# A two-layer decoder trunk on one core: feature stages that begin on two turned tiles, mixer output kept in SBUF, and the last chunk computed half by half

## The chip, the cores and the metric

The kernel runs on one core of one Trainium2 chip. The metric is the time of one execution in device microseconds (us). The kernel before was run three times: 2418.59 us median, 2418.29 to 2418.76. Results differ by less than 0.02% from run to run here.

## The reference, cut to what matters

The input is one sequence of 256 tokens, 2048 wide, f32. Two layers follow one another, and each is three residual steps, every one with an RMS norm before it and one behind it:

```
for i in range(2):
    hn = rms_norm(h, pre_mix_g[i])
    y = conformer_conv(hn, ...) if i == 0 else diff_attention(hn, ...)
    h = h + rms_norm(y, post_mix_g[i])
    f = conv_ffn(rms_norm(h, pre_ffn_g[i]), ...)          # 2048 -> 2 x 5632 -> 2048
    h = h + rms_norm(f, post_ffn_g[i])
    gate = sigmoid(rms_norm(h, ple_pre_g[i]) @ w_gate[i] + b_gate[i])
    h = h + rms_norm(gate * (p[i] @ w_proj[i]), ple_post_g[i])
return h
```

All products are computed from f32 weights (some 447 MB are read) to nearly f32 accuracy.

## The kernel before, in words

**Products.** A weight unit is 256 rows by 512 columns. SyncE loads it into one of four raw slots (RING = 4). ScalarE casts it to `w_hi` (`split` of the scalar block, L625), VectorE makes the rest `w_lo = raw - w_hi` (`split` of the vector block, L1021), and TensorE multiplies three times: high by high, high by low, low by high. A unit that has been multiplied frees its slot (`units_used`). The activations `x` have a high and a low part too.

**Two kinds of stage.** In a token stage (pw2, wo, down, gate, gates) the output has tokens on partitions: per unit two halves of 128 tokens with six matmuls each (`token_unit`, L1642 to L1644), and 8 units (22 in down) fill the two banks of a chunk of 512 columns. In a feature stage (up0, qk, up1) the output has features on partitions: `feature_chunk` with `product(j)` runs over the 8 units j of a chunk, each with 2 input tiles kt and 4 feature blocks, 16 matmuls in all (L1607 and L1609), into four of the eight PSUM banks, 0 to 3 for the first chunk.

**The turn into a stage.** The stages come one after the other and each starts from the new `h`. At the end of a mixer or embedding step, ScalarE sums squares (L663), VectorE applies the bias (L1120) and the gain (`times_gain`, L1058) and reduces the sums (L1037, L1039), and GpSimd takes the power -1/2 (L561). Then `residual` on VectorE updates `h` in eight pieces of 128 tokens by 512 columns (L1066), TensorE turns `h` into 16 tiles of 128 features by 256 tokens in PSUM (`turn_h`, L1587, two transposes of 128x128 a tile), ScalarE makes the high parts (`x_high`, L655), and VectorE the low parts (`x_low`, L1046). There are three turns into a feature stage: mix0 to up0, ple0 to qk, mix1 to up1. In these tile kt lies at position kt, two to a bank, so tiles 0 to 7 lie in banks 0 to 3, where the first chunk's products go. So the first chunk begins when four tiles are ready, multiplies two units for blocks 0 and 1 alone (their banks hold tiles 0 to 3), and goes on when eight tiles are ready:

```
early = 2
pe.wait_ge(x_ready, KT * LEFT[left] + 4)
for j in range(early):
    product(j, (0, 1))
```

Tiles 8 to 15 are turned inside the first chunk, after product 1 (mix) or 2 (qk). The mixer's chunk 0 of output is kept in SBUF (`y_first`) and its other three chunks stay in PSUM until the residual has read them. While the norm is worked out, `keep_warm` runs 17 (mix0) or 13 (mix1) small matmuls on TensorE (L1699).

**The statistic.** The norm's scale is applied after the product, so the stage begins without it. The squares of `h` (`h_squares`, L647) are summed on ScalarE, VectorE reduces them (`inverse_root`), GpSimd takes the root, VectorE writes two diagonals (`rstd_diagonals`, L1107), and TensorE spreads them over all partitions (`spread_statistic`, L1594), after product 5 in the up stages and after product 6 in qk. `turn_p` (L1904) turns the rows of p after product 4. All these stand in the engines' queues, in the order in which `new_h` (mix to up) and `new_h_behind` (ple0 to qk) write them, between the casts and splits of units 3 to 7.

**The end.** In the last gate chunk (gates1) both halves of a unit are multiplied before the next unit. Then `gate_post` works on halves 0 and 1, both roots are taken in one instruction, and of the eight pieces of the output five are updated on VectorE (`ON_DVE`, L1066) and three on TensorE and ScalarE (`ON_PE` = 3, 5, 7: `ident` by `h` plus `diag` by `z`, L1957 and L1962, copied at L1002). SyncE (L536) and ScalarE (L1004) issue a store of 256 KB for each piece. Ten more keep-warm matmuls (END_WARM) stand before the diagonals' products.

## Time and profile before

| what | us |
|---|---|
| median of 3 runs | 2418.59 |
| the profiled execution's own time | 2418.1 |
| its span, first to last instruction | 2416.3 |
| TensorE busy | 2398.6 (99%) |
| VectorE busy | 1638.4 (68%) |
| ScalarE busy | 1238.3 (51%) |

A timeline's row gives start, duration, engine, line, operation, the tiles written and read, how many instructions it merges (x8), and in brackets the idle time of the engine before it with what ended it. "issue" there means that nothing in the profile shows what the engine waited for. PE is TensorE, DVE VectorE, ACT ScalarE, POOL GpSimd, SPq and ACTq the queues that issue DMAs. Merged instructions overlap: the last of x8 ends at the row's end, and the step from one to the next is (duration - one instruction) / 7.

### The profile page before, as it was taken

What the parts mean: (1) busy time and instruction counts of PE and PEld (TensorE: products, weight loads), DVE (VectorE), ACT (ScalarE), POOL (GpSimd) and SP (SyncE); (2) the same over time, 40 slices, a digit from 0 to 9 for tenths busy, and PEclk for the clock granted to TensorE, in tenths of its full rate; (3) what the DMA queues carried; (4) which work ended last, traced back from release to release, by engine and by line L of the source; (5) the groups of instructions that cost most, each with busy time, mean ns of one, the idle gap of its engine ahead of it and who ended that gap; (6) DMA issues with size and microseconds to landing.
All of it is one profiled execution on the core that took longest, in us unless ns stands there. A gap on an engine that the chain in (4) does not pass through costs nothing.

```text
span 2416.3 us, 38816 instructions
## 1 busy us (share of the span) xinstructions
PE 2398.6 (99%) x12372; PEld 2057.9 (85%) x12372; DVE 1638.4 (68%) x2223; ACT 1238.3 (51%) x1777; POOL 36.1 (1%) x65
## 2 busy tenths in 40 slices
PE   9999999999999999999999999999999999999999
PEld 8888788888888888888888888888888888888887
DVE  6999767777777754447755676577777777644475
ACT  3433645555555544446644455465656656444463
POOL 2000000000000000000000000000000000000000
PEclk9999999999999999999999999999999999999999
DMA  8552546656656665566576544646566656656563
GB/s 268 181 165 90 175 148 205 187 180 198 191 182 191 196 209 195 193 199 227 176 212 201 183 150 156 193 155 192 183 190 196 187 182 197 212 187 200 194 234 135
DMA packets 370942, 452.48 MB, mean 187 GB/s; under 512 B 27460, under 2 KB 279494, under 8 KB 369440
## 3 DMA queue, kind: packets, MB, share of 16 engines
q1 hardware_dynamic: 367456, 435.54, 56.8%
q0 software_dynamic: 2960, 15.02, 1.8%
q8 instruction: 44, 0.72, 0.1%
q10 hardware_dynamic: 432, 0.79, 0.1%
q14 instruction: 50, 0.41, 0.1%
HBM read 447.05 MB, written 4.19 MB: 187 GB/s over the span
## 4 chain that ended last, share of the span: by engine, by line
PE 94%; issue 3%; DVE 1%; ACT 0%; DMA 0%; SPq 0%; POOL 0%; ACTq 0%; POOLq 0%; DVEq 0%
PE ps L1607 31%; PE ps L1609 16%; PE ps L1642 12%; PE ps L1643 12%; PE ps L1644 12%; PE ps L1692 9%; PE ps L1587 1%; PE ps L1856 0%; PE ps L1842 0%; DVE h L1066 0%; PE ps L1785 0%; PE ps L1793 0%; DMA h<-in_x 0%; PE ps L1572 0%; POOL rstd L561 0%
## 5 line engine op out<-in xcount | busy, mean ns | idle before, releaser
L1021 DVE TENSOR_TENSOR w_lo<-raw,w_hi 128x1024 fp32r<-128x1024 f32 x758 | 923.6, 1224 | 627.7 <-ACT w_hi L625 621.8
L625 ACT CAST w_hi<-raw 128x1024 fp32r<-128x1024 f32 x758 | 791.0, 1049 | 721.6 <-PE ps L1644 365.7
L1607 PE MATMUL ps<-x,w_hi 128*128 128x512 f32 x3328 | 1155.5, 391 | 4.1 <-issue 4.1
L1609 PE MATMUL ps<-x,w_lo 128*128 128x256 f32 x3328 | 931.7, 280 | 0.0
L1607 PEld LDWEIGHTS ps<-x,w_hi 128*128 128x128 f32 x3328 | 622.4, 187 | 141.2 <-issue 4.7
L1609 PEld LDWEIGHTS ps<-x,w_lo 128*128 128x128 f32 x3328 | 628.9, 189 | 0.0
L1644 PE MATMUL ps<-w_hi,mid 128*128 128x512 f32 x704 | 273.9, 389 | 0.0
L1643 PE MATMUL ps<-w_lo,mid 128*128 128x512 f32 x704 | 273.9, 389 | 0.0
L1642 PE MATMUL ps<-w_hi,mid 128*128 128x512 f32 x704 | 273.9, 389 | 0.0
L1642 PE MATMUL ps<-w_hi,x 128*128 128x512 f32 x640 | 253.2, 396 | 0.0
L1644 PE MATMUL ps<-w_hi,x 128*128 128x512 f32 x640 | 249.3, 389 | 0.0
L1643 PE MATMUL ps<-w_lo,x 128*128 128x512 f32 x640 | 249.2, 389 | 0.0
L1692 PE MATMUL ps<-xn,wg 128*128 128x256 f32 x896 | 193.7, 379 | 0.0
L1692 PEld LDWEIGHTS ps<-xn,wg 128*128 128x128 f32 x896 | 170.2, 190 | 23.1
L1462 DVE SCALAR_TENSOR_TENSOR acc<-ext,cols,acc 128x256 f32<-128x256 f32 x352 | 147.2, 480 | 46.0 <-ACT acc L931 39.6
L1644 PEld LDWEIGHTS ps<-w_hi,mid 128*128 128x128 f32 x704 | 132.2, 188 | 27.7
L1642 PEld LDWEIGHTS ps<-w_hi,mid 128*128 128x128 f32 x704 | 132.2, 188 | 27.4
L1643 PEld LDWEIGHTS ps<-w_lo,mid 128*128 128x128 f32 x704 | 132.2, 188 | 27.2
L1644 PEld LDWEIGHTS ps<-w_hi,x 128*128 128x128 f32 x640 | 120.1, 188 | 25.3
L1642 PEld LDWEIGHTS ps<-w_hi,x 128*128 128x128 f32 x640 | 120.2, 188 | 25.0 <-issue 0.4
L1643 PEld LDWEIGHTS ps<-w_lo,x 128*128 128x128 f32 x640 | 120.2, 188 | 24.5 <-issue 0.2
L1188 DVE SCALAR_TENSOR_TENSOR acc<-u_ext,wconv,acc 128x256 f32<-128x256 f32 x322 | 133.9, 477 | 1.2 <-ACT acc L750 1.1
(193 smaller groups left out, 1297.7 us busy)
## 6 DMA issues: line engine op xcount, KB each, us to landing
raw<-in_ffn_w_in SPq DMA_DIRECT2D x704, 256.0 KB, 3.2
raw<-in_ffn_w_out SPq DMA_DIRECT2D x352, 256.0 KB, 3.5
raw<-in_attn_w_qkv SPq DMA_DIRECT2D x192, 256.0 KB, 2.9
raw<-in_ple_w_gate SPq DMA_DIRECT2D x128, 256.0 KB, 3.7
wg<-in_conv_w_pw SPq DMA_DIRECT2D x112, 256.0 KB, 3.9
raw<-in_conv_w_pw SPq DMA_DIRECT2D x64, 256.0 KB, 3.6
raw<-in_attn_w_o SPq DMA_DIRECT2D x64, 256.0 KB, 3.5
wg<-in_conv_w_pw SPq DMA_DIRECT2D x32, 128.0 KB, 4.2
```

What stands on the lines that cost most here:

```text
L625: nc.scalar.copy(w_hi[:, u % RING], raw[:, u % RING]).then_inc(hi_split, 1)
L1021: nc.vector.tensor_tensor(w_lo[:, u % RING], raw[:, u % RING], w_hi[:, u % RING].bitcast(F32), ALU.subtract).then_inc(split_done, 1)
L1188: step.mark(nc.vector.scalar_tensor_tensor(both[:, a], u_ext[:, p, tap:tap + T], wconv[:, tap * KT + p:tap * KT + p + 1], nshift[:] if tap ...
L1462: ins = nc.vector.scalar_tensor_tensor(acc[:, f], ext[:, f, tap:tap + T], col(f"ffn_tap{layer}{tap}", c * 2 + (f if f < 2 else FT + f - 2) ...
L1587: ins = nc.tensor.transpose(tiles[:, turned_at(left, kt), P * half:P * (half + 1)], h[:, half, P * kt:P * (kt + 1)], ident[:])
L1607: mm(ps[:, 4 * s + f], w_hi[:, u % RING, q, columns], x[:, kt].rearrange("p a t -> p (a t)"), start=kt == 0, stop=False)
L1609: ins = mm(ps[:, 4 * s + f, 0:T], w_lo[:, u % RING, q, columns], x[:, kt, 0], start=False, stop=kt == KT - 1)
L1642: mm(bank(half), hi, w_hi[:, u % RING, q], start=first, stop=False)
L1643: mm(bank(half), hi, w_lo[:, u % RING, q], start=False, stop=False)
L1644: ins = mm(bank(half), lo, w_hi[:, u % RING, q], start=False, stop=last)
L1692: ins = mm(ps[:, 4 * (c % 2) + f, 0:T], wg[:, glu_slot(u), q, P * f:P * (f + 1)], source[:, kt], start=kt == 0, stop=kt == KT - 1)
```

## The change

Feature stages (mix0 to up0, ple0 to qk, mix1 to up1; the set `ALONE`):
- Tiles 0 to 11 lie one to a bank in banks 4 to 7, and tiles 12 to 15 in banks 4 and 5. Tiles 4 to 7 use the places of 0 to 3, tiles 8 to 11 again the same.
- The first residual chunk is done in four instructions of 256 columns instead of two of 512; TensorE turns tiles 0 and 1, then 2 and 3 (`turn_begun`). Product 0 waits for two ready tiles, and product j for 2j+2. There is no early part any more.
- The other tiles are turned in three groups of four inside the first chunk, behind products 0, 2 and 4 (`turn_rest`), each once the places are free.
- `new_h` becomes `new_h_quick` with another order of residuals, low parts, squares, casts and splits, and qk uses it too. In up stages `turn_p` moves behind product 5.
- All of the mixer's output goes to SBUF (`y_mix`). In pw2's last chunk VectorE leaves two splits, not one, for behind the chunk.
- The early projections of layer 1 use banks 0 to 3, and both are copied before the stage begins. MIX_WARM is (15, 13).

The kernel's end:
- The last four units of the last chunk are multiplied for half 0 first, then for half 1.
- Sigmoid, gating, squares, root, diagonal and residuals are done for half 0, then for half 1. Two roots of one column each replace one of two. The gain's product is written to `sig`.
- `ON_PE` is (0, 2, 1), `ON_DVE` is (4, 6, 3, 5, 7), and END_WARM is gone.

```diff
             if left in ALONE:
+                return 8 + 2 * (kt % 4) if kt < 12 else kt - 4
...
+            def residual_begun(source):
+                for q in range(UNIT_N // PAIR_N):
+                    columns = slice(PAIR_N * q, PAIR_N * (q + 1))
+                    for half in range(HALVES):
+                        nc.vector.scalar_tensor_tensor(h[:, half, columns], source(0, half)[:, columns], rstd[:, half:half + 1],
+                                                       h[:, half, columns], ALU.mult, ALU.add).then_inc(h_updated if q else h_begun, 1)
...
+            def new_h_quick(source, left, scale, first, done):          # vector block
...
+                residual_begun(source)
+                x_low(left, scale, range(0, 2))
+                residual(source, range(2, 3))
+                x_low(left, scale, range(2, 4))
+                ahead(1)
+                residual(source, range(3, 4))
+                ahead(2)
+                x_low(left, scale, range(4, 8))
+                ahead(3)
+                residual(source, range(4, 6))
+                ahead(4)
+                residual(source, range(6, PIECES))
+                x_low(left, scale, range(8, 12))
+                ahead(5)
+                x_low(left, scale, range(12, KT))
+                ahead(6)
                 dve.wait_ge(hstats_done, PIECES * (HNORM[left] + 1) + 1)
                 inverse_root(hstat, D)
+                ahead(7)
                 dve.wait_ge(rstd_ready, stats[0])
...
+            def new_h_quick(add, left, scale, first, cast):             # scalar block
...
+                x_high(left, scale, range(0, 4))
+                ahead(2)
+                h_squares(left, add, range(0, 3))
+                x_high(left, scale, range(4, 8))
+                ahead(3)
+                h_squares(left, add, range(3, 4))
+                ahead(4)
+                h_squares(left, add, range(4, 6))
+                x_high(left, scale, range(8, 12))
+                ahead(5)
+                h_squares(left, add, range(6, 7))
+                x_high(left, scale, range(12, KT))
+                ahead(6)
+                h_squares(left, add, range(7, PIECES))
+                ahead(7)
...
+            def turn_rest(add, j):
+                if j in (0, 2, 4):
+                    c = j // 2 + 1
+                    pe.wait_ge(x_ready, KT * LEFT[BECOMES[add]] + (4, 8, 10)[j // 2])
+                    turn_h(add, range(c, c + 1))
...
                 for j in range(UPC):
                     if i is None and n == 0:
-                        pe.wait_ge(x_ready, KT * LEFT[left] + max(2 * j + 2, KT // 2))
-                    product(j, (2, 3) if j < early else (0, 1, 2, 3)).then_inc(units_used, 1)
+                        pe.wait_ge(x_ready, KT * LEFT[left] + 2 * j + 2)
+                    product(j).then_inc(units_used, 1)
                     if between is not None:
                         between(j)
...
                 def embedding_rows(j):
-                    if j == 1:
-                        turn_h(f"mix{layer}", range(NC // 2, NC))
-                    if j == 4:
+                    turn_rest(f"mix{layer}", j)
+                    if j == 5:
                         turn_p(layer)
-                    if j == 5:
                         spread_statistic(6, (3, 5)[layer])
...
+            for j in range(UPC - RING):
+                pe.wait_ge(split_done, is_split(first + j))
+                token_unit(first + j, bank, (2 * j, 2 * j + 1), x, j == 0, False)
+            for half in range(HALVES):
+                for j in range(UPC - RING, UPC):
+                    pe.wait_ge(split_done, is_split(first + j))
+                    half_unit(first + j, bank, (2 * j, 2 * j + 1), x, False, j == UPC - 1, half)
             for k, n in enumerate(ON_PE):
                 _, half, columns = piece(n)
                 mm(ps[:, k], ident[:], h[:, half, columns], start=True, stop=False)
-            keep_warm(END_WARM, len(ON_PE))
-            pe.wait_ge(diag_ready, 12)
-            for k, n in enumerate(ON_PE):
-                _, half, columns = piece(n)
+                pe.wait_ge(diag_ready, 11 + half)
                 mm(ps[:, k], diag[:, half], z[:, half, columns], start=False, stop=True).then_inc(sums_made, 1)
...
+                    gated_half(0, lambda: None)
+                    root_of(0)
+                    residual(last_piece, ON_DVE[0:1])
+                    gated_half(1, lambda: residual(last_piece, ON_DVE[1:2]))
+                    root_of(1)
+                    residual(last_piece, ON_DVE[2:])
```

`ahead(k)` casts or splits unit k of the first chunk unless it was done before: in the scalar block for k from 4 (up) or 2 (qk), in the vector block for k from 2 (up0), 1 (qk) or 3 (up1). `gated_half(half, meanwhile)` is gate, bias, `meanwhile`, product with z, product with the gain, and the reduced square of one half; `root_of(half)` waits for the root and writes the diagonal of that half.

## Rows read from the trace of the kernel before

**Rows 1.** The page: busy time of TensorE, VectorE, ScalarE, and the chain's shares.

```profile
PE 2398.6 (99%) x12372; PEld 2057.9 (85%) x12372; DVE 1638.4 (68%) x2223; ACT 1238.3 (51%) x1777; POOL 36.1 (1%) x65
PE 94%; issue 3%; DVE 1%; ACT 0%; DMA 0%; SPq 0%; POOL 0%; ACTq 0%; POOLq 0%; DVEq 0%
```

**Rows 2.** The waits of TensorE over the whole span: total us, times, longest.

```profile
PE ps L1607 <- issue: 4.1, 3, 1.4
```

**Rows 3.** Timeline, turn mix0 to up0, up to the first product.

```profile
339.96 1.23 DVE L1021 TENSOR_TENSOR w_lo<-raw,w_hi 128x1024 fp32r<-128x1024 f32 x1 [1.50 <-ACT w_hi L625]
340.94 0.39 PE L1643 MATMUL ps<-w_lo,x 128*128 128x512 f32 x1
341.10 1.29 DVE L1120 TENSOR_TENSOR ps<-ps,bias 128x512 f32<-128x512 f32 x2
341.17 0.39 PE L1644 MATMUL ps<-w_hi,x 128*128 128x512 f32 x1
343.57 0.16 DVE L1037 TENSOR_REDUCE ssum<-stat 128x2 f32<-128x8 f32 x1 [0.20 <-ACT y_sink L663]
344.02 0.71 POOL L561 TENSOR_TENSOR rstd<-meansq,minus_half 128x2 f32<-128x2 f32 x1 [71.96 <-DVE meansq L1039]
344.88 1.41 DVE L1066 SCALAR_TENSOR_TENSOR h<-y_first,rstd,h 128x512 f32<-128x512 f32 x2 [0.34 <-POOL rstd L561]
347.26 3.03 ACT L655 ACTIVATE x<-ps,cols 128x256 fp32r<-128x256 f32 x8 [2.79 <-PE ps L1587]
348.13 3.23 DVE L1046 SCALAR_TENSOR_TENSOR x<-ps,cols,x 128x256 fp32r<-128x256 f32 x8 [0.52 <-ACT x L655]
349.89 0.47 PE L1607 MATMUL ps<-x,w_hi 128*128 128x512 f32 x1 [1.35 <-issue]
```

**Rows 4.** Timeline, first chunk of up0, up to the statistic.

```profile
355.52 1.91 PE L1587 MATMUL ps<-ident,h 128*128 128x128 f32 x16
359.47 2.04 ACT L625 CAST w_hi<-raw 128x1024 fp32r<-128x1024 f32 x2
363.85 0.63 ACT L647 ACTIVATE h_sink<-h 128x512 f32<-128x512 f32 x1
365.55 2.36 DVE L1021 TENSOR_TENSOR w_lo<-raw,w_hi 128x1024 fp32r<-128x1024 f32 x2 [0.58 <-ACT w_hi L625]
367.82 0.48 DVE L1107 TENSOR_SCALAR diag<-ident,rstd 128x128 f32<-128x128 f32 x2
368.97 0.60 PE L1594 MATMUL ps<-diag,ones 128*128 128x128 f32 x4
```

**Rows 5.** Timeline, the turns ple0 to qk and mix1 to up1: first residual, statistic.

```profile
1182.28 2.74 DVE L1066 SCALAR_TENSOR_TENSOR h<-z,rstd,h 128x512 f32<-128x512 f32 x4 [0.66 <-POOL rstd L561]
1208.55 0.60 PE L1594 MATMUL ps<-diag,ones 128*128 128x128 f32 x4
1571.31 1.42 DVE L1066 SCALAR_TENSOR_TENSOR h<-y_first,rstd,h 128x512 f32<-128x512 f32 x2 [0.31 <-POOL rstd L561]
1595.51 0.60 PE L1594 MATMUL ps<-diag,ones 128*128 128x128 f32 x4
```

**Rows 6.** Timeline, the kernel's end.

```profile
2403.09 0.75 DVE L1122 SCALAR_TENSOR_TENSOR sig<-ps,rstd,bias 128x512 f32<-128x512 f32 x1 [0.54 <-PE ps L1644]
2406.49 1.07 POOL L561 TENSOR_TENSOR rstd<-meansq,minus_half 128x2 f32<-128x2 f32 x1 [74.20 <-DVE meansq L1039]
2408.06 3.40 DVE L1066 SCALAR_TENSOR_TENSOR h<-z,rstd,h 128x512 f32<-128x512 f32 x5
2408.84 3.11 SPq L536 DMA_DIRECT2D out<-h  x5
2412.02 0.34 ACTq L1004 DMA_DIRECT2D out<-h  x1
```

**Rows 7.** Windows at the end; the last three columns: clock, DMA share, GB/s.

```profile
2410.00:2411.00 1.00, 1.00 (x3) 0.19 (x1) 1.00 (x3) 0.59 (x1) 0.00 (x0) 1.00 1.04 381
2414.60:2414.90 0.30, 0.00 (x0) 0.00 (x0) 0.00 (x0) 0.00 (x0) 0.00 (x0) 0.55 1.05 376
```

More of the change, by code:

```diff
@@ L120, in trunk @@
     HNORM = {"mix0": 0, "ffn0": 1, "ple0": 2, "mix1": 3, "ffn1": 4, "ple1": 5}
-    ON_PE = (3, 5, 7)
-    ON_DVE = tuple(n for n in range(PIECES) if n not in ON_PE)
+    ON_PE = (0, 2, 1)
+    ON_DVE = (4, 6, 3, 5, 7)
     BLOCKS, PV_LAG = HEADS * HALVES, 6
@@ L652, in x_high, with y_squares @@
                 for kt in kts:
-                    if kt % 4 == 0:
-                        act.wait_ge(turned, PIECES * (LEFT[left] - 1) + kt // 2 + 2)
+                    if kt % 2 == 0:
+                        act.wait_ge(turned, PIECES * (LEFT[left] - 1) + kt // 2 + 1)
                     nc.scalar.activation(x[:, kt, 0], tiles[:, turned_at(left, kt)], ACT.Copy, scale=scale(kt)).then_inc(x_hi, 1)
-            def y_squares(k, source, c, made):
-                for half in range(HALVES):
+            def y_squares(k, source, c, made, halves=range(HALVES)):
+                for half in halves:
                     made(half)
@@ L985, in post @@
                         squares(c)
-                    chunk(i, UPC, place[f"gates{layer}"] + (0 if i is not None else UPC * (c - 1)), post, tail)
+                    chunk(i, UPC, place[f"gates{layer}"], post)
                 def first_post():
@@ L997, in _ @@
                 if last:
-                    gate(None, NC - 1, tail=RING)
+                    split(None, 0, place[f"gates{layer}"] + UPC * (NC - 2) + RING, UPC - RING)
+                    for half in range(HALVES):
+                        sigmoid(NC - 1, (half,))
+                        squares(NC - 1, (half,))
                     for k, n in enumerate(ON_PE):
@@ L1022, in split, with chunk @@
                                             ALU.subtract).then_inc(split_done, 1)
-            def chunk(i, first, post, last=False, done=0):
-                split(i, UPC, first + RING + done, UPC - 1 - done)
+            def chunk(i, first, post, last=False, done=0, behind=1):
+                split(i, UPC, first + RING + done, UPC - behind - done)
                 post()
                 if not last:
-                    split(i, UPC, first + RING + UPC - 1, 1)
+                    split(i, UPC, first + RING + UPC - behind, behind)
             def col(name, k=0):
@@ L1314, in token_stage @@
                 with dve.Fori(0, NC - 1 - peeled) as i:
-                    step.enter(i, HALVES)
                     chunk(i, place[name] + UPC * peeled, lambda: post(i, i + 1 if peeled else i))
-                    step.leave(NC - 1 - peeled)
-                chunk(None, place[name] + UPC * (NC - 1), lambda: post(None, NC - 1), True)
-            token_stage("pw2", "mix0", biases=True, done=2)
+                chunk(None, place[name] + UPC * (NC - 1), lambda: post(None, NC - 1), True, behind=behind)
+            token_stage("pw2", "mix0", biases=True, done=2, behind=2)
             z_pieces = lambda c, half: z[:, half, UNIT_N * c:UNIT_N * (c + 1)]
@@ L1573, in turn, with turn_begun @@
                     ins.then_inc(turned, HALVES)
+            BECOMES = {"mix0": "ffn0", "ffn0": "ple0", "ple0": "mix1", "mix1": "ffn1", "ffn1": "ple1"}
+            def turn_begun(add):
+                for q in range(UNIT_N // PAIR_N):
+                    for half in range(HALVES):
+                        if q:
+                            pe.wait_ge(h_updated, PIECES * ADD[add] + half + 1)
+                        else:
+                            pe.wait_ge(h_begun, HALVES * QUICK[add] + half + 1)
+                        for kt in (2 * q, 2 * q + 1):
+                            ins = nc.tensor.transpose(tiles[:, turned_at(BECOMES[add], kt), P * half:P * (half + 1)],
+                                                      h[:, half, P * kt:P * (kt + 1)], ident[:])
+                    ins.then_inc(turned, 1)
             def turn_h(add, chunks):
-                left = {"ffn0": "ple0", "ffn1": "ple1"}.get(add)
+                left = BECOMES[add]
                 for c in chunks:
```

175 lines of the change are left out of this document (95 added, 80 removed).

## The prediction

> **What bounds the kernel now.** I read the page first. TensorE is busy for 2398.6 of 2416.3 us, and the chain that ended last runs through it for 94% of the span [rows 1]. Next I read TensorE's waits. The largest entry is three waits of 1.4 us before the feature product L1607 [rows 2], one for each turn into a feature stage; none stands inside a stage. So time can be won only at these turns and in the tail behind the last matmul, and whatever makes TensorE wait inside a first chunk is lost one for one. Then I read the timeline of the turn mix0 to up0 [rows 3, 4]. From the last matmul of pw2 (starts 341.17) to the first product (349.89) pass 8.7 us: bias, squares, root, residual, transposes, high parts, low parts. In the chunk that follows I looked for the second deadline, the statistic. Its diagonals are done at 367.82 + 0.48 = 368.30, and TensorE asks for them at 368.97 [rows 4]. They are 0.7 us early, and that is all the slack there is.
>
> **The sum is made** against the profiled execution: 2418.1 us, of which 2416.3 are span and 1.8 lie around it. That is 0.5 below the median of 2418.59, and I add the 0.5 back at the end. A change of less than 0.2% (4.8 us) I call no change.
>
> **Part 1, the start of a feature stage.** I count t from the first residual instruction: 344.88, 1182.28, 1571.31 [rows 3, 5]. Durations: eight low parts take 3.23, so 0.40 a step and 0.43 for the last; eight high parts 3.03, 0.37 a step [rows 3]; sixteen transposes 1.91, 0.11 a step; a unit's product (355.52 - 349.89) / 2 = 2.82 [rows 3, 4]. The trace has no residual of 256 columns. From above it costs what one of 512 does, a step of 0.67 [rows 3]; from below half of that, 0.33. I take the step 0.40 of the nearest row, the low part of the same form and width, and 0.48 to its end.
> - Before: first product at t = 5.01.
> - After: residual quarters done at 0.48, 0.88, 1.28, 1.68. Tiles 0 and 1 are turned at 1.33, tiles 2 and 3 at 2.13. High parts begin at 1.39; low part 0 at 1.89, low part 1 ends at 2.72. Product 0 starts at 2.8, 2.2 us sooner (1.2 with the dear residual, 2.4 with the cheap one).
> - Paid back: the eight transposes of tiles 4 to 7 stood in the gap, and now stand between products: 8 x 0.11 = 0.9.
> - Net 1.3 sooner. TensorE reaches the statistic of an up stage at 2.8 + 6 x 2.82 + 3 x 0.9 + 0.4 (turn_p, four transposes) = 22.8, where before it was there at 24.1.
>
> **Part 2, the statistic.** It now hangs on tiles 12 to 15, which are turned behind product 4. That product ends at 2.8 + 5 x 2.82 + 2 x 0.9 = 18.7, the transposes at 19.6. On ScalarE follow in its queue the four high parts (19.8 to 21.3), the cast of unit 6 (1.0, to 22.3 [rows 4]), the last square (0.63 [rows 4]) and the cast of unit 7 (22.9 to 23.9). VectorE has before the diagonals the split of unit 6 (22.4 to 23.5, 1.14 a step [rows 4]), the reduction (0.3), and the split of unit 7, which must wait for that cast: 24.0 to 25.1. GpSimd's root lies beside it. The diagonals take 0.48 [rows 4], so they are ready at 25.6. TensorE waits from 22.8 to 25.7: **a new stall of 2.9 us, which eats the 1.3 won and 1.6 more.** ScalarE and VectorE had nothing to do from about 16.5 to 19.7, but they cannot use it, since the next tiles aren't turned yet.
> - up0: statistic at 25.7 for 24.1, +1.6. up1: at 25.7 for 1595.51 - 1571.31 = 24.2, +1.5 [rows 5].
> - qk: the statistic stands behind product 6, so there TensorE first waits for the split of unit 6. VectorE has one more split in this queue (unit 1) and ScalarE two more casts (2, 3); by the same steps this split ends at 23.9, product 6 at 26.7, for 1208.55 - 1182.28 = 26.3 before: +0.5. The copies of both early projections end at about 1183.5, before the first high part (1183.7), so they cost nothing.
> - Behind the statistic, chunk 1 needs its units 6.0 us later in both kernels, and all engines have moved along with TensorE. Nothing more is lost, nothing won back.
> - Bounds of the three together: each step of the chain from product 4 to the diagonals is a row, so I allow 0.5 us a stage: +2 to +5.
>
> **Part 3, pw2's last chunk.** The bias of its first half waited for a split (339.96 to 341.10) [rows 3] while its product was complete at about 340.2. With that split put off, first bias 340.3, second bias when the last matmul has ended, 341.6 for 341.7; ScalarE's second square no longer queues behind the first, and the reduction comes at 343.1 for 343.57: -0.5. Output to SBUF instead of PSUM, first chunk's gain: same count and width, 0. The two fewer warm matmuls only fill that shorter gap.
>
> **Part 4, the end.** The last matmul ends at 2403.05 as before, since the same matmuls run in another order. Half 0 is complete 24 matmuls earlier, 24 x 0.227 = 5.4 (two in a row start at 340.94 and 341.17 [rows 3]; the unit of twelve takes 2.72), at 2397.6, and its gate, root and diagonal (5 us) and one residual lie beside TensorE's work, until 2403.3. That is 0.15 past the last matmul, so half 1 starts its gate 0.15 late. Half 1's chain to the root is as long as before (2403.09 to 2406.49 [rows 6]), then the root takes 1.07 as here [rows 6] or 0.71 as at 344.02 [rows 3]. The call for half 0 has just run the same code, so I take 0.7. Diagonal at 2407.7; then three residuals instead of five behind two diagonals (3.40 for five, 0.66 a step [rows 6]): last one at 2409.8. One piece instead of three goes over TensorE and ScalarE, issued at about 2409.6. The last store is issued at 2409.9 where it was 2412.02 [rows 6].
> Before, the eight stores of 256 KB begin at 2408.84 and then keep the DMA engines full at 381 GB/s [rows 6, 7]: 2.1 MB are 5.5 us, and the span ends 1.0 behind them. Now four have left before 2408.2, and four remain: bytes from 2409.3, 2.75 us, 2412.1, and 1.0: 2413.1. **-3.1.** Bounds: -1.8 (only the last issue comes sooner, and the root takes 1.07) and -3.6.
>
> **Sum:** +1.6 - 0.5 + 0.5 + 1.5 - 3.1 = 0.0. 2418.1, and 2418.6 against the median. What the end wins, the late statistic takes.
>
> **A rule against this change.** Before, TensorE's longest wait at a turn was 1.4 us [rows 2], and the granted clock is full in every slice up to the end. After the last work, busy until 2411 or so, the clock is down to its half level (1.2 of 2.4 GHz) in the stretch 2414.6 to 2414.9 [rows 7]. So an idle stretch of 1.4 us costs no clock, one of 3.6 does, and the new one of 2.9 lies between. The Trainium skill (TensorE: Matmul & The Clock Gate, section on the HAM clock gate) says that the array's default is the half rate, and that only activity lifts it. By that rule each new stall could be followed by products at half speed; by the rows up to 1.4 us it is free. I take it as free, since 2.9 is still short of 3.6, and price the other below.
>
> **The rivals.**
> - *The statistic is in time.* If the diagonals are there by t = 22.8, every turn keeps its 1.3 (1.1 in qk, whose arrival would be 25.2): -1.3 - 0.5 - 1.1 - 1.4 - 3.1 = -7.4, **2411.2**. For it: the whole change is built around the earlier start. Against it: it would need four engines' steps to be 2.8 us shorter than rows of the same form. Chance 0.10.
> - *The clock falls in the new stall* (the slower side). Place: products 6 and 7 of up0 and up1, behind the stall of 2.9. If the level drops, these take 5.6 instead of 2.8: 2 x 2 x 2.8 = 11.3, **2429.9**. It decides once the stall lasts longer than the chip grants, somewhere between 1.4 and 3.6. Against it: 2.9 is the one idle stretch of its kind, with full work on both sides. Chance 0.06.
> - *The end pays little.* If the last stores are slow for themselves and not because eight are in line, the end gives 1 and the sum is +2.1: **2420.7**, still no change. For it: a single store's landing has a floor that I cannot see in the rows. Chance 0.10.
> - *The forecast*: 2416.6 to 2420.4 by the bounds above. Chance 0.74.
>
> **Numbers.** Predicted 2418.6. The range goes from 2414.0 (a statistic half as late with a good end) to 2421.5 (the third rival and a margin), and leaves out the first two rivals and some 0.03 beside them. Faster by over 0.2% (under 2413.8): the first rival and a little, 0.12. Slower by over 0.2% (over 2423.4): 0.07. The same: 0.81.
>
> **What would show it.** In the timeline of up0, the first product 2.8 us behind the first residual instruction, L1594's counterpart at 25.7 with a wait of some 2.9 on the diagonals before it, the same in up1; in qk a wait of 1.3 on the split of unit 6. In TensorE's waits, the diagonals' entry grows from nearly nothing to about 6 us, and the three entries before L1607 shrink. The reduction of mix0 comes 0.5 sooner. The span ends 10.1 us behind the last weight matmul, where it was 13.3. A statistic without a wait would make the forecast wrong on the fast side; a granted clock under 1.00 behind the stalls on the slow side.

## The result, and the profile after

| | before | after |
|---|---|---|
| median of 20 executions each | 2418.24 us | 2426.63 us |
| fastest and slowest | 2417.51, 2420.90 | 2420.75, 2446.53 |
| ratio after to before, of the means | | 1.0044, 95% interval 1.0030 to 1.0058 |
| profiled execution, its span | 2418.1, 2416.3 | 2432.4, 2430.6 |

The changed kernel is slower by 0.44% by the means and by 0.35% by the medians, where no change was predicted (2418.6, up to 2421.5), and it has become uneven. The twenty executions after don't scatter round one value: one is at 2420.8, eight lie at 2422.9 to 2424.7, two at 2426.5 and 2426.8, seven at 2431.1 to 2434.2, and two at 2444.7 and 2446.5. The large groups stand some 9 us apart, and the last one some 12 above that. Before, all twenty lie within 3.4 us (0.14%, and not the 0.02% of the first three). The profiled execution after is one of the group at 2432. One execution of e15 below (2994 us, granted clock 0.752) was disturbed and is left out.

The page's busy times and chain, after (answer to [rows 1]):

```profile
PE 2410.9 (99%) x12348; PEld 2060.0 (85%) x12348; DVE 1640.2 (67%) x2231; ACT 1238.3 (51%) x1777; POOL 39.2 (2%) x66
PE 97%; DVE 1%; issue 1%; SPq 0%; DMA 0%; POOL 0%; ACT 0%; DVEq 0%; POOLq 0%; ACTq 0%
```

TensorE has 24 instructions fewer, all of them warm-ups, and is yet busy for 12.3 us longer. Waits alone don't do that. TensorE's waits, after (answer to [rows 2]):

```profile
PE ps L1690 <- DVE diag L1156: 7.2, 3, 3.5
PE ps L1703 <- issue: 1.5, 2, 0.7
PE ps L1703 <- DVE w_lo L1045: 1.2, 1, 1.2
PE ps L1703 <- DVE x L1072: 0.9, 1, 0.9
```

The three waits of 1.4 us before the first products have shrunk to 0.7 to 0.9, and the wait for the statistic's diagonals has appeared at 3.5 us in up0 and 3.3 in up1, with 1.2 on a split in qk. The timeline of the turn mix0 to up0, after (answer to [rows 3, 4]; start, duration, then the instruction):

```profile
343.05 0.16 DVE L1061 TENSOR_REDUCE ssum<-stat 128x2 f32<-128x8 f32 x1 [0.29 <-ACT y_sink L672]
344.36 1.67 DVE L1101 SCALAR_TENSOR_TENSOR h<-y_mix,rstd,h 128x256 f32<-128x256 f32 x4 [0.36 <-POOL rstd L566]
347.25 0.47 PE L1703 MATMUL ps<-x,w_hi 128*128 128x512 f32 x1 [0.73 <-issue]
...
368.11 1.23 DVE L1045 TENSOR_TENSOR w_lo<-raw,w_hi 128x1024 fp32r<-128x1024 f32 x1
368.14 1.75 POOL L566 TENSOR_TENSOR rstd<-meansq,minus_half 128x2 f32<-128x2 f32 x1 [23.93 <-DVE meansq L1063]
369.92 0.70 DVE L1156 TENSOR_SCALAR diag<-ident,rstd 128x128 f32<-128x128 f32 x2 [0.58 <-POOL rstd L566]
370.68 0.71 PE L1690 MATMUL ps<-diag,ones 128*128 128x128 f32 x4 [3.48 <-DVE diag L1156]
```

The reduction is 0.52 sooner, the first product comes 2.89 behind the first residual instruction (predicted 2.8), and the statistic 26.3 behind it (predicted 25.7, before 24.1). The other turns, after (answer to [rows 5]):

```profile
1194.70 1.28 DVE L1101 SCALAR_TENSOR_TENSOR h<-z,rstd,h 128x256 f32<-128x256 f32 x3 [0.66 <-POOL rstd L566]
1222.84 0.60 PE L1690 MATMUL ps<-diag,ones 128*128 128x128 f32 x4
1585.60 0.48 DVE L1101 SCALAR_TENSOR_TENSOR h<-y_mix,rstd,h 128x256 f32<-128x256 f32 x1 [0.32 <-POOL rstd L566]
1611.76 1.01 PE L1690 MATMUL ps<-diag,ones 128*128 128x128 f32 x3 [3.27 <-DVE diag L1156]
```

The ledger against the rows of before, as the lead or lag of each event: first residual of mix0 -0.5; statistic of up0 +1.7; first residual of ple0 **+12.4**; statistic of qk +14.3; first residual of mix1 +14.3; statistic of up1 +16.3; last weight matmul +17.7; end of the span +14.3. So 10.7 us are lost between the statistic of up0 and the first residual of ple0, where TensorE never waits in either kernel and the change touches nothing. Two more views say what they are. The clock, in windows of after (TensorE busy and its instructions, granted clock, DMA share, GB/s):

```profile
372.00:375.40 3.40, 3.40 (x13) 0.52 0.56 193
1198.20:1201.60 3.40, 3.40 (x13) 0.50 0.55 203
1611.20:1614.50 3.30, 2.74 (x10) 0.50 0.82 261
```

TensorE runs at half level (1.2 of 2.4 GHz) for 3.4 us behind each stall of an up stage and once at the sparse start of qk. A stretch of 3.4 us at half rate does the work of 1.7, so each costs 1.7 us. That explains 1.7 of the 10.7. The other 9.0 are in the rate of the products. First after, a stretch of up0 (400 to 800 us) and the one of up1 that answers to it (1640 to 2040), then before, 400 to 800 (x is how many, then busy us and mean ns):

```profile
L1703 PE MATMUL ps<-x,w_hi 128*128 128x512 f32 x1134 | 400.7, 399 | 0.0
...
L1703 PE MATMUL ps<-x,w_hi 128*128 128x512 f32 x1155 | 400.4, 391 | 0.0
```

```profile
L1607 PE MATMUL ps<-x,w_hi 128*128 128x512 f32 x1155 | 400.4, 391 | 0.0
```

In 400 us at full granted clock and without an idle moment, up0 of after makes 1134 products of 512 columns, up1 and the kernel before 1155. The same pair of matmuls (512 columns with the high weights, 256 with the low) has **two rhythms**. Worked out from the first and last start of a stage's products behind chunk 0, a pair takes 346.67 ns or 353.33 ns to within 0.1, and nothing between. From start to start the quick one steps 347, 347, 346 or 344, 350 (two forms with the same mean), the slow one 350, 349, 361. Inside the first chunk the rhythm changes at interruptions; behind it a stage keeps what it has to its end. An up stage has some 1360 pairs behind the statistic, so the slow rhythm costs it 1360 x 6.67 ns = 9.1 us; qk, with some 460, 3.0. The groups of executions fit this: from 2423.7, qk slow gives 2426.7, one up stage slow 2432.8, and all three stages 2444.9. Only one execution has a profile, so for the others this is worked out and not read.

The tail, after (answer to [rows 6, 7]):

```profile
2420.76 0.75 DVE L1606 SCALAR_TENSOR_TENSOR sig<-ps,rstd,bias 128x512 f32<-128x512 f32 x1 [0.48 <-PE ps L1732]
2424.12 0.55 POOL L566 TENSOR_TENSOR rstd<-meansq,minus_half 128x1 f32<-128x1 f32 x1 [4.82 <-DVE meansq L1618]
2426.83 0.34 ACTq L1028 DMA_DIRECT2D out<-h  x1
...
2427.00:2428.00 1.00, 0.00 (x0) 0.00 (x0) 0.00 (x0) 0.00 (x0) 0.00 (x0) 1.00 1.02 373
```

From the last gate's start to the last issue pass 6.1 us, where it was 8.9; the lag falls from 17.7 to 14.3, a gain of 3.4.

The gain's product now runs beside neither root. In the kernel before it did, and its root took 1.07 us. In that kernel's timeline this row stands just ahead of the root:

```profile
2406.32 0.68 DVE L1058 TENSOR_TENSOR z<-z,gain 128x512 f32<-128x512 f32 x1
```

Both its inputs lie in SBUF, and the root ends 0.56 us behind it. Where the gain's product reads PSUM instead (the root at 344.02, [rows 3]), the root beside it takes 0.71.

### The profile page after: what moved, and what is told of

Read it like the earlier page. It is cut to its first block, busy times and chain, and to the rows that moved or that the text cites. A ratio compares the mean times of both kernels' runs of the same rounds, so it can differ in the third digit from the quotient of the medians.

```text
span 2430.6 us, 38776 instructions
## 1 busy us (share of the span) xinstructions
PE 2410.9 (99%) x12348; PEld 2060.0 (85%) x12348; DVE 1640.2 (67%) x2231; ACT 1238.3 (51%) x1777; POOL 39.2 (2%) x66
## 4 chain that ended last, share of the span: by engine, by line
PE 97%; DVE 1%; issue 1%; SPq 0%; DMA 0%; POOL 0%; ACT 0%; DVEq 0%; POOLq 0%; ACTq 0%
PE ps L1703 32%; PE ps L1705 16%; PE ps L1732 13%; PE ps L1730 13%; PE ps L1731 13%; PE ps L1785 9%; PE ps L1675 1%; PE ps L1949 0%; PE ps L1935 0%; SPq L477 0%; PE ps L1878 0%; DMA h<-in_x 0%; POOL rstd L566 0%; DVE x L1072 0%; PE ps L1886 0%
## 5 line engine op out<-in xcount | busy, mean ns | idle before, releaser
L1045 DVE TENSOR_TENSOR w_lo<-raw,w_hi 128x1024 fp32r<-128x1024 f32 x758 | 923.8, 1223 | 634.2 <-ACT w_hi L634 632.6
L1703 PE MATMUL ps<-x,w_hi 128*128 128x512 f32 x3328 | 1168.7, 396 | 3.5 <-issue 1.5
```

Of the source, the lines that this page charges most:

```text
L1045: nc.vector.tensor_tensor(w_lo[:, u % RING], raw[:, u % RING], w_hi[:, u % RING].bitcast(F32), ALU.subtract).then_inc(split_done, 1)
L1703: mm(ps[:, 4 * s + f], w_hi[:, u % RING, q, columns], x[:, kt].rearrange("p a t -> p (a t)"), start=kt == 0, stop=False)
```

## The experiments

Fifteen kernels. A product of unit j is called product j; "slow" and "quick" are the two rhythms. A ratio is that of the means, against the kernel before in the same batch. The first four ask which part of the change costs what.

**e1_warm_stall.** In the stalls of the up stages TensorE gets work:

```diff
+                        keep_warm(14, 6)
                         spread_statistic(6, (3, 5)[layer])
```

> The changed kernel, with 14 keep-warm matmuls (0.23 us each) on TensorE in bank 6 before its wait for the diagonals in up0 and up1, so that it works through the stall instead of standing. Theory 1 (the stall drops the clock, and the recovery in the middle of the stream can leave the matmuls in a slower rhythm for the rest of the stage): no half-rate stretch in up0 and up1, 1.7 us back at each, no slow rhythm behind them; all runs within about 1.5 us of 2420, but for one that may be 3.5 higher by qk. Theory 2 (the slow rhythm comes from the new order of the first chunk, not from the clock): 3.4 us back, but runs still scatter between 2420 and 2440. Theory 3 (the clock has no part, the records only show it): no change, 2423.6 and up.

Measured: 2431.09 us (2422.93 to 2433.35, 6 executions), ratio 1.0042. The windows of e1 behind both stalls:

```profile
372.00:376.00 4.00, 4.00 (x25) 1.00 0.63 202
1611.00:1615.00 4.00, 4.00 (x24) 1.00 0.97 303
```

In the profiled execution the clock no longer falls anywhere, but four of six executions are above 2430, and in the profiled one qk and up1 have the slow rhythm. So the falls of the clock aren't what makes the rhythm, nor most of the loss.

**e2_turn_early.** The turns behind products 0, 2, 3 (in `turn_rest`):

```diff
-                if j in (0, 2, 4):
-                    c = j // 2 + 1
-                    ... (4, 8, 10)[j // 2])
+                if j in (0, 2, 3):
+                    c = (j + 1) // 2 + 1
+                    ... (4, 8, 10)[c - 1])
```

> The changed kernel with the last group of tiles turned behind product 3 instead of 4. Theory 1 (the statistic is late because tiles 12 to 15 are turned late): the diagonals come 2.8 us sooner, the stall of 3.4 us in up0 and up1 shrinks to about 0.6, the wait for the split of unit 6 in qk goes, and with the stalls the two falls of the clock: 2423.6 - 2.9 - 2.8 - 1.2 - 3.4 = about 2413.3, runs close together. Theory 2 (slow rhythm by the new order): the same gain for the best run, but runs up to 9 or 18 us higher. Rival 3 (ScalarE's or VectorE's queue is the limit, not the turning): the stall stays above 2 us, 2420 or more.

Measured: 2426.32 us (2412.86 to 2431.67, 12 executions), ratio 1.0026: two at 2412.9 and 2413.8, four at 2420.8 to 2422.7, six at 2429.9 to 2431.7. The stall shrinks as computed (to 0.5 us) and the clock stays up, but over the base stand zero, one or two steps of 9 us.

**e3_root_alone.** The diagonals ahead of the split of unit 7 (the two later calls of `rstd_diagonals`, not shown, go):

```diff
                 inverse_root(hstat, D)
-                ahead(7)
                 dve.wait_ge(rstd_ready, stats[0])
+                rstd_diagonals()
+                ahead(7)
```

> The changed kernel with the two diagonals written before VectorE's split of unit 7 instead of behind it, so that no split runs beside GpSimd's root. Theory 1 (the root took 1.75 us instead of 0.70 because VectorE's split ran beside it): root 0.70 us, diagonals 1.0 to 1.2 us sooner, stall 2.3 instead of 3.4; 2421.2 if the clock still falls, 2417.8 if a stall of 2.3 us no longer drops it. Rival (the root is slow after the long idle time of GpSimd, whatever VectorE does): root 1.75 again, diagonals at most 0.5 us sooner.

Measured: 2434.20 us (2423.50 to 2441.97, 6 executions), ratio 1.0064. The root of up0 in e3:

```profile
368.13 0.69 POOL L566 TENSOR_TENSOR rstd<-meansq,minus_half 128x2 f32<-128x2 f32 x1 [23.94 <-DVE meansq L1063]
```

0.69 with VectorE idle, where the changed kernel took 1.75 with a split started 0.03 ahead. That split ends at 368.11 + 1.23 = 369.34, and the root 0.55 later, which fits GpSimd standing until the split has ended. The Trainium skill (SBUF — State Buffer, who interferes with whom) says that a VectorE instruction with two inputs in SBUF and a GpSimd instruction that reads SBUF exclude each other, and the later one waits for the whole of the other; where GpSimd is the later one these traces agree (the roots beside such an instruction end 0.55 to 0.57 us behind it in both kernels). The stall is 2.4 us in up0 and 2.2 in up1 instead of 3.5 and 3.3, and the clock still falls behind both.

**e4_new_end_alone.** The kernel before with the change's end by halves, and nothing else of it (`ON_PE`, `ON_DVE`, one root a half, `half_unit`, `gated_half`).

> The kernel before with the new end alone (last four units half by half, ON_PE and ON_DVE of the change, no END_WARM). All theories: the tail behind the last weight matmul shrinks by 3.4 us, 2418.2 - 3.4 = 2414.8, runs as close together as those of before (within 1 us). If the scatter came from the end, this one would scatter too; a time of 2417 or more would say that part of the tail's gain in the changed kernel is only the delay before it.

Measured: 2415.16 us (2414.16 to 2418.74, 11 executions), ratio 0.9987, interval 0.9979 to 0.9996. Span 2413.3, 3.0 less than before. The end is worth what it was said to be, and none of e4's executions has a step of 9 us.

**e5_early_and_alone.** e2 and e3 together. **e6_burst.** The changed kernel with `keep_warm(6, 5)` behind product 7 of each up stage.

> The changed kernel with both earlier edits: the turns of the later halves of h behind products 0, 2 and 3, and the diagonals of the root made before the split of unit 7, so that TensorE waits for the first statistic by under 0.3 us where the changed kernel waits 3.5 us. Theory A (a wait of TensorE in the first chunk is what lets a stage fall into the slow rhythm of its products, 353.3 ns a pair in place of 346.7 ns): the stages of the up projection keep the quick rhythm as in the kernel before, and nearly all executions are at 2411 to 2414 us, with at most the 3.4 us of the qk stage above that. Theory B (the rhythm is drawn by the new pattern of turns, short interruptions of eight transposes each, whether TensorE waits or not): the executions lie at about 2412, 2421 and 2430 us as they did with the turns early alone, median above 2418. Reading of its profile under both: no stretch at half clock behind the statistic, GpSimd's root 0.7 us.

> The changed kernel with six matmuls of 128x128 more at the end of the first chunk of each up stage, into a free bank, behind product 7: one more interruption of the products, that TensorE reaches at full clock and without a wait. Cost of the matmuls themselves about 0.6 us per stage. Theory A (a wait of TensorE before the last interruption lets the slow rhythm in; an interruption reached without one gives the quick rhythm, as in the kernel before): both up stages are quick, the executions are at 2422 to 2426 us, none at 2431 or above. Theory B (every interruption of this kernel draws anew, by whatever phase the products had): the executions scatter over 9 us as in the changed kernel. A further outcome, that the rhythm set by the wait passes through the interruption unchanged, would look the same as theory B in the times, and in the profile would show the same rhythm ahead of and behind the six matmuls.

e5: 2430.67 us (2427.99 to 2433.38, 5 executions), ratio 1.0049. TensorE waits 0.4 us in all for diagonals, none of it in a feature stage, and the clock is full, yet all three stages of its profiled execution are slow. A wait isn't needed for the slow rhythm: theory A in its plain form falls. e6: 2438.36 us (2424.77 to 2446.81, 6 executions), ratio 1.0084, one up stage slow and one quick in the profile. Six matmuls reached without a wait don't mend it.

**e7_p_beside.** The kernel before, the rows of the embedding behind product 5:

```diff
-                    if j == 4:
-                        turn_p(layer)
                     if j == 5:
+                        turn_p(layer)
                         spread_statistic(6, (3, 5)[layer])
```

> The kernel before with one move of the change: the four transposes of the embedding rows behind product 5, right ahead of the statistic, where they stood behind product 4. No wait is added. Theory A (waits): as the kernel before, 2418 to 2419 us, all executions within 1 us but for the 3.4 us steps that the kernel before has too. Theory B in the form that two interruptions together, in place of two with a product between, let the slow rhythm in: steps of 9 us above 2418 in a third or more of the executions.

Measured: 2436.26 us (2427.30 to 2437.48, 5 executions), ratio 1.0075, interval 1.0062 to 1.0088. This is the plainest run of the study. It has the old kernel's instructions, all of them, with four transposes of 0.11 us one product later, no new wait, a full clock, and 18 us more. (The profiled execution is the one at 2427.3, with up0 slow and up1 quick; the other four, at 2435.7 to 2437.5, have no profile and fit two slow up stages.) So the short turns of eight transposes aren't needed either: theory B as e5 put it falls, and the form put ahead of e7, two interruptions together, came true. The interruption of e7 in up0, and the products behind it (400 to 800 us):

```profile
368.22 0.40 PE L1607 MATMUL ps<-x,w_hi 128*128 128x512 f32 x1
368.45 0.28 PE L1609 MATMUL ps<-x,w_lo 128*128 128x256 f32 x1
368.57 0.60 PE L1904 MATMUL ps<-ident,p_rows 128*128 128x128 f32 x4
369.01 0.61 PE L1594 MATMUL ps<-diag,ones 128*128 128x128 f32 x4
369.37 0.48 PE L1607 MATMUL ps<-x,w_hi 128*128 128x512 f32 x1
```

```profile
L1607 PE MATMUL ps<-x,w_hi 128*128 128x512 f32 x1133 | 400.4, 399 | 0.0
```

From product to product across it pass 1.15 us, and the slow rhythm follows.

**e8_old_start_waits.** The kernel before with `spread_statistic` behind product 4, with the rows.

> The kernel before with the statistic moved one product forward, behind product 4: its diagonals come when product 5 would be nearly done, so TensorE waits for them some 2 us in each up stage, in the otherwise old order. Theory A (the wait lets the slow rhythm in): the wait costs about 2 us per stage, half of the executions or more carry steps of 9 us above 2422, up to 2440. Theory B (the new pattern of turns is what does it): 2422 to 2424 us, without steps of 9 us. If the clock falls in the stall, 1.7 us more for each fall under both.

Measured: 2439.01 us (2426.11 to 2444.85, 6 executions), ratio 1.0074. In the profile both up stages are slow, with waits of 2.2 and 2.0 us and one fall of the clock. It has both a wait and the rows beside the statistic, so it doesn't tell the two apart.

The last two interruptions of the first chunk were now the suspects: theory C, that the statistic must stand alone, a product behind the rows.

**e12_early_as_before.** e5 with these two where the kernel before has them:

```diff
-                    if j == 5:
+                    if j == 4:
+                        pe.wait_ge(x_ready, KT * LEFT[f"ffn{layer}"] + 12)
                         turn_p(layer)
+                    if j == 5:
                         spread_statistic(6, (3, 5)[layer])
```

> The changed kernel with turns behind products 0, 2 and 3, diagonals before the split of unit 7, the embedding rows turned behind product 4 and the statistic behind product 5: the last two interruptions stand as in the kernel before, with one whole product between them. TensorE waits for nothing by more than 0.7 us. Theory C (what the last interruption of the first chunk looks like sets the rhythm: the statistic's two matmuls alone, a whole product behind the transposes of the rows, give the quick rhythm; rows and statistic in one interruption may give either): the up stages are quick, the executions lie at 2410 to 2415 us. Theory B (the short turns of eight transposes draw the rhythm): as the kernel with both earlier edits, 2428 to 2433 us, or scattered in steps of 9 us below that.

Measured: **2410.67 us** (2410.08 to 2412.76, 11 executions), ratio 0.9961, interval 0.9947 to 0.9976. It beats both kernels in every execution, without a step. The interruption of e12 in up0, and the products behind it (400 to 800 us):

```profile
365.19 0.69 POOL L566 TENSOR_TENSOR rstd<-meansq,minus_half 128x2 f32<-128x2 f32 x1 [21.20 <-DVE meansq L1063]
366.55 0.40 PE L1702 MATMUL ps<-x,w_hi 128*128 128x512 f32 x1
366.78 0.28 PE L1704 MATMUL ps<-x,w_lo 128*128 128x256 f32 x1
366.90 0.61 PE L1689 MATMUL ps<-diag,ones 128*128 128x128 f32 x4
367.26 0.47 PE L1702 MATMUL ps<-x,w_hi 128*128 128x512 f32 x1
```

```profile
L1702 PE MATMUL ps<-x,w_hi 128*128 128x512 f32 x1155 | 400.4, 393 | 0.0
```

0.71 us across the statistic, and quick. Against e5 it moves four transposes by one product (with the `x_ready` wait shown, at which TensorE doesn't stand) and gains 20 us.

**e10_early_apart**, **e9_apart**, **e11_old_apart_late.** Rows behind product 5, statistic behind product 6, in e5, in the changed kernel and in the kernel before.

> The changed kernel with the turns early, the diagonals before the split of unit 7, rows behind product 5, statistic alone behind product 6. Theory C: quick up stages, 2410 to 2415 us, and at most the 3.4 us of the qk stage above. Theory B: steps of 9 us above 2412 in half of the executions or more.

> The changed kernel with the one edit that the statistic stands behind product 6 in the up stages, the rows stay behind product 5. The stall of 3.5 us is covered by product 6 (2.8 us), 0.7 us is left in each up stage, the clock does not fall there. Theory C: 2412 to 2416 us, no steps of 9 us. Theory B: the same base with steps of 9 us, median above 2420.

> The kernel before with the rows behind product 5 and the statistic behind product 6: the same two interruptions with a product between, each one product later. Theory C (what stands together decides): as the kernel before, 2418 to 2419 us. If instead the exact place in the chunk decides (the phase in which TensorE's products are then), steps of 9 us in some executions, as with rows and statistic together.

Measured: e10 2430.14 us (2421.21 to 2431.27, 12 executions), ratio 1.0030; e9 2422.07 (2415.94 to 2426.43, 12), ratio 1.0003; e11 2437.53 (2419.70 to 2439.56, 12), ratio 1.0054; all three in steps. Theory C as I had put it misses in all three. Their traces show what I had overlooked: the statistic stands alone, with 713 to 716 ns across it (725 in e9's up1), but it isn't the last interruption. Chunk 1 now starts with a wait of 1.3 us for a split in up1 (L1045, L1021 in e11), and with a hitch of some 50 ns in up0 (402 to 406 ns from product to product), which no other kernel has there. In five of these six stages the products between the statistic and chunk 1 run in the quick rhythm; four of the five are slow behind the hitch or the wait, and only e11's up0 stays quick.

That led to theory D: the last interruption of the stage's start decides, and it is safe if it has the statistic's own length and TensorE doesn't wait at it. Three runs tested that.

**e13_as_before_alone.** The changed kernel with e12's edit alone, stall kept. **e15_early_late_root.** e12 without e3's edit, so with a short wait.

> The changed kernel with the places of the kernel before for the last two interruptions of an up stage's first chunk (rows behind product 4, statistic behind product 5), and nothing else: the root still comes late, so TensorE waits for it by 3.5 to 4.5 us, and the clock falls behind it. Theory C alone (the statistic by itself with a whole product ahead of it is enough): quick up stages, 2420 to 2424 us, no steps of 9 us. Theory D (an interruption gives the quick rhythm only if the statistic stands alone and TensorE does not wait at it: the gap of 712 to 714 ns that all nineteen such stages had that were quick): the executions scatter in steps of 9 us from 2421, as the changed kernel's.

> The quick version with rows behind product 4 and the statistic behind product 5, but with the diagonals behind the split of unit 7 as the change has them: turns behind 0, 2, 3. TensorE then waits about 1 to 1.5 us for the statistic in each up stage, the clock does not fall. Theory D: the wait lets the slow rhythm in, steps of 9 us above 2413 in half of the executions. Theory C alone: 2412 to 2415 us in all.

e13: 2423.67 us (2420.97 to 2443.43, 11 executions), ratio 1.0042: six at 2421.0 to 2423.7, four at 2430.1 to 2434.4, one at 2443.4. The place alone isn't enough while TensorE waits there. e15: 2412.43 us (2411.71 to 2426.39, 11 executions), ratio 0.9989, interval 0.9976 to 1.0002: eight executions at 2411.7 to 2414.6 and three at 2421.2 to 2426.4; waits of 0.7 us at the most, where 1 to 1.5 were expected. Three in eleven have a step where e12, without the wait, has none in eleven. That is less often than expected and points to the short wait, but eleven executions each are few.

**e14_two_behind.** The changed kernel, stall and all, with one more interruption as long as the statistic's:

```diff
                     if j == UPC - 1:
+                        keep_warm(2, 5)
```

> The changed kernel with two matmuls of 128x128 more behind product 7 of each up stage, as long as the statistic's own and reached without a wait: a last interruption of the form that was followed by the quick rhythm wherever it came behind products of 350 ns. The stall and the falls of the clock stay. Theory D: the gap is 712 to 714 ns and the up stages are quick, 2421 to 2424 us (0.3 us for the matmuls), unless products 6 and 7 already ran at 347 ns, where the gap was 710 ns twice and the rhythm slow behind it. Theory B (any draw, the form of the interruption does not matter): scatter in steps of 9 us as the changed kernel and as with six matmuls there.

Measured: 2426.98 us (2424.44 to 2427.80, 5 executions), ratio 1.0034. No execution has a step of 9 us, and both up stages of the profile are quick. Of the changed kernel's twenty, nine had a step, so five without one would come by chance about once in twenty times. The added interruption in e14's up0:

```profile
379.37 0.40 PE L1703 MATMUL ps<-x,w_hi 128*128 128x512 f32 x1
379.60 0.28 PE L1705 MATMUL ps<-x,w_lo 128*128 128x256 f32 x1
379.72 0.61 PE L1792 MATMUL ps<-ident 128*128 128x128 f32 x4
380.08 0.47 PE L1703 MATMUL ps<-x,w_hi 128*128 128x512 f32 x1
```

0.71 us from product to product again. In both up stages product 7, ahead of the two added matmuls, runs in the slow rhythm (349, 350, 361), and the products behind them in the quick one (350, 344). The times are some 3 us above the expected ones; in the profiled execution the clock stayed down for 6.8 us behind each stall and not 3.4, which makes 3.4 us of it.

**All profiled stages together.** Seventeen profiles have 51 feature stages. Sorted by the gap between the starts of two 512-column products across the last interruption at the stage's start (in the up stages of e9 to e11 the hitch or wait ahead of chunk 1):

| last interruption | stages | quick | slow |
|---|---|---|---|
| the statistic or its like alone, no wait, gap 712 to 714 ns | 22 | 22 | 0 |
| the same in qk, gap 710 ns | 2 | 0 | 2 |
| the same in qk, gap 725 ns | 1 | 0 | 1 |
| any other: longer, with a wait, or a hitch | 26 | 12 | 14 |

One more reading of the same starts says why a short interruption matters. The first chunk of a stage has several interruptions, and between them the products already run in one of the three step patterns. Across a lone statistic (or the two added matmuls of e14) reached without a wait, the pattern changes in a fixed way:

| gap, ns | pattern ahead | pattern behind | times |
|---|---|---|---|
| 712 to 714 | 350, 344 (quick) | 347, 347, 346 (quick) | 13 |
| 712 to 714 | 350, 349, 361 (slow) | 350, 344 (quick) | 13 |
| 710 | 347, 347, 346 (quick) | slow | 2 |
| 716 | 350, 344 (quick) | 350, 344 (quick) | 1 |
| 725 | slow | slow | 2 |

These are 31 and not 25, since the statistics of e9 to e11 are counted here too. The rows' four transposes standing alone take the stream from 350, 344 to slow (seven times, gaps of 704 and 705 ns), from slow to 350, 344 (three times, 721) or leave it slow (twice, 706). So in the kernel before, up0 goes slow, rows, 350/344, statistic, 347; in e12 it goes 350/344, rows, slow, statistic, 350/344. In both, the rows leave a pattern from which the statistic leads to a quick one. Rows and statistic in one interruption are one such step instead of two: in e5 both up stages go from 350/344 to slow, and in e7 up0 stays slow. The stream thus carries a state over a short interruption. This is read from the traces. The expectation of e14 had a part of it (quick behind products of 350 ns, slow behind 347), and e14 bore that part out; no run was built to test the rest of the table. What in TensorE holds such a state stays open, and so does why stages with a wait fall either way.

## Why the prediction was wrong, step by step

- **What bounds the kernel: incomplete.** "So time can be won only at these turns and in the tail behind the last matmul": TensorE's own rate inside a stage was taken as fixed. It is not, and this is where most of the loss in the profiled execution sits (9.0 of 14.3 us).
- **Part 1: right.** First product at 2.9 for 2.8 predicted.
- **Part 2, the stall: right, a little short.** 3.5 and 3.3 us for 2.9; qk 1.2 for 1.3. The missing 0.6 is the root for the most part: I laid it beside the split ("GpSimd's root lies beside it") at 0.7, and it took 1.75, because it stood until the split had ended, so VectorE stood idle for 0.58 behind the split. The diagonals, 0.70 for 0.48, are the rest. Statistics at +2.2, +1.9 and +2.0 us against the turns' first residuals, for +1.6, +0.5 and +1.5 predicted; in qk 1.7 of it is the clock.
- **Part 2, last point: the step that failed.** Of what lies behind the statistic I wrote "Nothing more is lost, nothing won back". Moving the rows beside the statistic and putting a wait there took away the interruption that had left the stages quick. It costs 9.1 us for each up stage that turns slow (by the groups of times, one or both did in nine of the twenty executions). e7 shows the loss without any other part of the change, and e12 against e5 shows it undone. Neither half is enough alone: e5 has no wait and is slow, e13 has the place and keeps the wait and still has steps. A slow qk costs 3.0; the change leaves qk's statistic behind product 6, and whether it makes a slow qk more frequent isn't shown (the kernel before has one execution of twenty some 3 us up too).
- **The clock: wrong side chosen, and the rival mis-sized.** I took the stall as free "since 2.9 is still short of 3.6". A wait of 2.4 us in e3 lost the clock too, and so did nine of the twelve stalls of 2.0 us or more in the profiles. The rival's price of 5.6 us a stage took two whole products at half rate, where 3.4 us at half rate cost 1.7. Three falls give 5.1 us: the group at 2422.9 to 2424.7 is the forecast plus 5, if its executions have the three falls of the profiled one. The Trainium skill's rule that full rate has to be earned by activity (TensorE: Matmul & The Clock Gate, the HAM clock gate) was the better guide than my bound from two idle stretches.
- **Part 3: right.** -0.52 for -0.5.
- **Part 4: right, with a wrong reason for one term.** -3.4 for -3.1, and in e4 alone -3.1 against the median. I took 0.7 and not 1.07 for the root because "The call for half 0 has just run the same code"; but the root of half 0 itself, the first one there, took 0.55 as well. The 1.07 of before goes with VectorE's product beside it, by the rows of the tail above.
- **The first rival was priced right.** "The statistic is in time: 2411.2." e12 makes it so and has 2410.67.
- **The range** held only waits, and its upper end was added up short: the bounds given for the parts (+5, -0.5, -1.8) make 2421.3, not the 2420.4 of the forecast's line. With clock falls and a slow stage the cases reach to 2446; no term of mine stood for a step of 9 us.

## What to carry to other kernels

Where a long stream of equal matmuls fills TensorE, look at start to start of the same instruction in both traces, not only at the waits: 2% of rate over 1400 pairs is more than any stall at a turn. What interrupts such a stream last matters beyond its own length, so place small work (a statistic, a few transposes) so that TensorE reaches it without a wait, read the step pattern on both sides of it, and compare several executions for steps before trusting a place. And a small GpSimd instruction on the critical path should not start while a VectorE instruction with two SBUF operands is running.

## What the hardware showed that I had not expected

- Two rhythms of one instruction stream at the same granted clock: 346.67 and 353.33 ns a pair, kept for over 470 us, chosen by an interruption that takes 0.4 us; and across a lone statistic reached without a wait, gap and pattern ahead together went with one pattern behind in all 31 cases.
- GpSimd's root of two columns: 0.69 to 0.73 us alone, 1.75 when a VectorE split of 1.23 had started 0.03 us ahead, 1.06 when a product of two SBUF operands (0.68) had started 0.18 ahead; of one column 0.55. A split that started 0.50 into the root (before, 365.55) took its usual 1.22.
- The half clock lasted 3.4 us at a time (6.8 in e14), and came behind nine of twelve waits of 2.0 to 3.5 us, so it isn't decided by the wait's length alone. Once (e10) it came at 247 us, far from every place of the change.
